# One block for the four mixer heads, and state space rows issued ahead

## The reference, cut to what matters

```
cum     = cumsum(dt * a)
h_new   = h * exp(cum[-1]) + B^T (exp(cum[-1] - cum) * xdt)
seg     = exp(where(lower, cum_i - cum_j, -inf))
y       = (C B^T * seg) xdt + (C h) * exp(cum)
```

```
rq, rk, rv, rg, gq, gk, gv, gz, ga, gb, gate_a, gate_b = split(xm @ w_in)
y_ret = silu(rg) * rms_norm(retention(rope(rq), rope(rk), rv))
q, k, v = silu(causal_conv(cat(gq, gk, gv), conv_w));  q, k = l2(q), l2(k)
A     = strict_lower(beta k k^T * decay) + I
per chunk:  v_new = A^-1 (beta v - beta exp(g) k S);  o = q exp(g) S + (q k^T * decay) v_new
            S = S * exp(g_last) + (k exp(g_last - g))^T v_new
y_gdn = rms_norm(o, norm_w) * silu(gz)
out   = (sigmoid(gate_a) * y_ret + sigmoid(gate_b) * y_gdn) @ w_out
```

## Time and profile before

| | us |
|---|---|
| median of three runs | 4228.22 |
| the profiled execution, own time | 4227.81 |
| its span, first to last instruction | 4225.5 |
| stage of the mixer heads, 2828.1 to 3604.9 | 776.8 |
| state space stage, from 1123 to 1718 | 595 |

### The profile page before, as it was taken

How to read it: one execution, slowest core, us unless ns; L and a number is a source line. 1 busy time by engine, 2 the same in 40 slices (tenths; PEclk the granted TensorE clock), 3 DMA queues, 4 the chain that set the end, 5 groups by cost and what they waited for, 6 DMA issues and landing times. The chain is left out here.

```text
span 4225.5 us, 56473 instructions
## 1 busy us (share of the span) xinstructions
PE 3428.7 (81%) x23892; PEld 2063.1 (49%) x23892; DVE 1546.8 (37%) x3163; ACT 916.8 (22%) x1817; POOL 53.6 (1%) x72
## 2 busy tenths in 40 slices
PE   5799999998698988699748787848888887659994
PEld 1466666666555544344333232334444444358883
DVE  2466666666345756100140000031413233241112
ACT  1243344342134446100110000011111212001001
POOL 0000000000000000000000000000000000000000
PEclk7899999999799998799859999959899999859997
DMA  3112212221222211420149999340111110247873
GB/s 135 46 56 71 71 56 71 71 70 55 73 70 68 67 63 50 176 100 0 73 187 391 428 428 428 142 164 3 80 40 42 40 43 0 85 158 293 326 317 150
DMA packets 109172, 548.20 MB, mean 130 GB/s; under 512 B 34336, under 2 KB 37136, under 8 KB 84512
## 3 DMA queue, kind: packets, MB, share of 16 engines
q1 hardware_dynamic: 102048, 519.97, 31.9%
q0 software_dynamic: 4608, 16.78, 1.1%
q10 hardware_dynamic: 2304, 8.39, 0.5%
HBM read 517.63 MB, written 27.47 MB: 129 GB/s over the span
## 5 line engine op out<-in xcount | busy, mean ns | idle before, releaser
L2066 PE MATMUL ex_ps<-ex_ring,ex_xs 128*64 128x512 f32 x1024 | 246.7, 639 | 62.1 <-DMA ex_ring<-expert_slabs_in 59.1
L571 PE MATMUL rw_ps<-hT,rw_w 128*128 128x512 f32 (+1 forms) x640 | 259.4, 535 | 16.4 <-DMA rw_w<-rw_slabs_in 16.1
L2803 PEld LDWEIGHTS ge_ps<-ge_xeT,ge_ring 128*128 128x128 f32 x2048 | 233.0, 193 | 10.5 <-issue 10.5
L2803 PE MATMUL ge_ps<-ge_xeT,ge_ring 128*128 128x128 f32 x2048 | 233.2, 276 | 2.9 <-DVE ge_xeT L2861 2.9
L2300 PE MATMUL mh_ps<-mh_w,xmT 128*128 128x512 f32 x512 | 221.5, 593 | 8.6 <-ACT mh_sg L2323 8.6
L2066 PEld LDWEIGHTS ex_ps<-ex_ring,ex_xs 128*64 128x64 f32 x1024 | 88.4, 147 | 219.9 <-issue 219.9
L1375 PE MATMUL sg_ps<-hTp,sg_w 128*128 128x512 f32 x384 | 174.4, 608 | 8.5 <-DMA sg_par<-conv_pars_in 8.5
L571 PEld LDWEIGHTS rw_ps<-hT,rw_w 128*128 128x128 f32 x640 | 113.4, 193 | 100.1 <-issue 73.8
L2300 PEld LDWEIGHTS mh_ps<-mh_w,xmT 128*128 128x128 f32 x512 | 97.0, 190 | 132.5 <-issue 120.5
L2291 PE MATMUL mh_ps<-xmT,mh_w_ahead 128*128 128x512 f32 x256 | 120.8, 636 | 22.8 <-PEq L61 22.8
L2066 PE MATMUL ex_ps<-ex_ring,ex_hidT 128*64 128x512 f32 x512 | 118.5, 617 | 14.2 <-DMA ex_ring<-expert_slabs_in 13.1
(11 more groups left out here) (568 smaller groups left out, 5538.8 us busy)
## 6 DMA issues: line engine op xcount, KB each, us to landing
ex_ring<-expert_slabs_in SPq DMA_DIRECT2D x96, 2048.0 KB, 19.8
ge_ring<-expert_slabs_in SPq DMA_DIRECT2D x48, 2048.0 KB, 12.3
rw_mod_w<-mod_w_in SPq DMA_DIRECT2D x64, 384.0 KB, 4.1
rw_mod_w<-ada_in SPq DMA_DIRECT2D x64, 256.0 KB, 3.3
sg_kern<-cum_dram SPq DMA_DIRECT2D x64, 256.0 KB, 3.2
mh_w_ahead<-head_slabs_in SPq DMA_DIRECT2D x8, 2048.0 KB, 10.0
mh_w<-head_slabs_in SPq DMA_DIRECT2D x8, 2048.0 KB, 10.0
rw_w<-rw_slabs_in SPq DMA_DIRECT2D x8, 1536.0 KB, 6.8
```

The source lines that it names most:

```text
L571: mm = pe.matmul(where[j, part], w[:, k, P * j:P * j + P], tokens, start=k == 0, stop=k == KC - 1)
L2066: mm = pe.matmul(ps[halves[j], bank, :], src[:, k, halves[j]], ring[:, (n + j) % RING, k, :], start=k == 0, stop=k == KC - 1)
L2803: mm = pe.matmul(ps[:, 2 + 2 * (j % 2) + n, P * f:P * f + P], w[:, k, P * f:P * f + P], xeT[:, j, k, :], start=k == 0, stop=k == KC - 1)
```

## The change

Two places.

In `ssm_branch` SP issues the first gate slab and the first five rows ahead of the passes. In pass c at step n it issues row 16c + n + 5 (the first whose buffer is then free), and the gate slab behind the row of step 1. Store and weight blocks keep their steps in the list.

`mixer_heads` becomes one block for the four heads; `mixer_head`, the hardware loop and the class `Inverse` are gone. Semaphores count on from head to head. The slabs go through a ring of two buffers. The arithmetic is the same; its order on the engines is new:
- token blocks alternate with turns, spread, products, scores and retention, so these are in the dense projection;
- the inverse has two pieces of two channel matmuls of the next head in each level, and the states have one such piece in each chunk; the taps for them are on VectorE in levels 3 to 6 (one behind the masks, one behind the subtracts), in chunk 2 and behind chunk 3;
- the gates are taken per token block, Silu, then Sigmoid;
- root and norm of the retention are ahead of the inverse; the norm row times the gate is between inverse and states;
- decay columns are read from `tok` without a copy; channel blocks use PSUM banks 5 and 6.

```diff
@@ ssm_branch, SP @@
+                sp.dma_start(wz[:, :, :], z_slabs[0]).then_inc(s.wz_in, 16)
+                for m in range(RING):
+                    load_rows(m)
                 for c in range(-1, SSM_G):
                     p = c + 1
-                    if p < SSM_G:
-                        if p:
+                    for n in range(16):
+                        if c >= 0 and 16 * c + n + RING < 16 * SSM_G:
+                            load_rows(16 * c + n + RING)
+                        if 0 < p < SSM_G and n == 1:
                             sp.wait_ge(s.z_done, nl * p)
-                        sp.dma_start(wz[:, :, :], z_slabs[p]).then_inc(s.wz_in, 16)
-                    for n in range(16):
-                        if c >= 0:
-                            load_rows(16 * c + n)
+                            sp.dma_start(wz[:, :, :], z_slabs[p]).then_inc(s.wz_in, 16)
@@ mixer_heads, SP @@
+                for n in range(2, 4 * HEADS):
+                    h, part = (n - 2) // 4, (n - 2) % 4
+                    if part == 0:
+                        sp.wait_ge(s.channel_major, 4 * h + 4)
+                    else:
+                        sp.wait_ge(s.token_major, 12 * h + 4 * part)
+                    sp.dma_start(w[:, n % 2, :, :], slabs[n]).then_inc(w_in[n % 2], 16)
+                    if part == 2 and h + 1 < HEADS:
+                        sp.wait_ge(s.scores_kept, 4 * h + 4)
+                        sp.dma_start(dec[:, :], decay[h + 1]).then_inc(s.dec_in, 16)
@@ TensorE @@
+                def channel(h, lo, hi):
+                    for j in range(lo, hi):
+                        b, k = j // KC, j % KC
+                        if j == 0 and h:
+                            pe.wait_ge(w_in[0], 32 * h)
+                            pe.wait_ge(s.token_kept, 12 * h)
+                        if k == 0 and b >= 2:
+                            pe.wait_ge(s.convolved, 4 * h + b - 1)
+                        mm = pe.matmul(ps[:, 5 + b % 2, :], w[:, 0, k, P * b:P * b + P], xmT[:, k, :], start=k == 0, stop=k == KC - 1)
+                        if k == KC - 1:
+                            mm.then_inc(s.channel_major, 1)
+                def invert(h, level):
...
+                        mm.then_inc(x_turned[k], 1)
+                    if more:
+                        channel(h + 1, 4 * level - 4, 4 * level - 2)
...
+                        mm.then_inc(y_product[k], 1)
+                    if more:
+                        channel(h + 1, 4 * level - 2, 4 * level)
...
+                        mm.then_inc(z_product[k], 1)
+                def chain(h, c):
...
+                    pe.matmul(ps[:, 1, 0:DV], mats[:, 0, c, :], rhs[:, :], start=True, stop=True).then_inc(s.v_done, 1)
+                    if h + 1 < HEADS:
+                        channel(h + 1, 24 + 2 * c, 26 + 2 * c)
+                    pe.wait_ge(s.v_ready, CH2 * h + c + 1)
...
+                channel(0, 0, 4 * KC)
+                for h in range(HEADS):
+                    token(h, 0)
+                    turn_channels(h)
+                    for n in range(1, 4):
+                        token(h, n)
+                    for n in range(3):
+                        turn(h, n)
+                    token(h, 4)
+                    turn(h, 3)
+                    turn(h, 4)
+                    token(h, 5)
+                    spread(h)
+                    token(h, 6)
+                    products(h)
+                    token(h, 7)
+                    scores(h, 0)
+                    scores(h, 1)
+                    token(h, 8)
+                    scores(h, 2)
+                    scores(h, 3)
+                    token(h, 9)
+                    retain(h, 0)
+                    retain(h, 1)
+                    token(h, 10)
+                    retain(h, 2)
+                    retain(h, 3)
+                    token(h, 11)
+                    pe.wait_ge(s.ret_kept, CH2 * h + CH2)
+                    for level in range(1, LEVELS_UP):
+                        invert(h, level)
+                    for c in range(CH2):
+                        chain(h, c)
@@ ScalarE, from the gates of block 9 on @@
+                    retain_square(h, 0)
+                    retain_square(h, 1)
+                    gates(h, 10)
+                    retain_square(h, 2)
+                    retain_square(h, 3)
+                    act.wait_ge(s.mean_r, h + 1)
+                    act.activation(ss2[:, 0, :], ss2[:, 0, :], ACT.Sqrt).then_inc(s.root_r, 1)
+                    gates(h, 11)
+                    for level in range(1, LEVELS_UP):
+                        for k in range(2):
+                            act.wait_ge(x_turned[k], N * h + level)
+                            act.copy(xx[:, k, :], ps[:, 2 * k, 0:2 * P]).then_inc(x_ready[k], 1)
+                        if more and level == 5:
+                            silu(h + 1, 0)
+                    if more:
+                        silu(h + 1, 1)
...
+                    act.activation(ss2[:, 1, :], ss2[:, 1, :], ACT.Sqrt).then_inc(s.root_g, 1)
+                    if more:
+                        silu(h + 1, 2)
+                        silu(h + 1, 3)
@@ VectorE @@
+                    for level in range(1, LEVELS_UP):
+                        level_up(h, level)
+                    dve.wait_ge(s.gated, 8 * h + 8)
+                    link(dve.tensor_tensor(gate_g[:, :, :], gate_g[:, :, :], per_unit(norm_w, CH2), ALU.mult))
+                    for c in range(CH2):
+                        chain(h, c)
+                        if more and c == 2:
+                            for i in range(4):
+                                tap(h + 1, 2, i)
+                    if more:
+                        for i in range(4):
+                            tap(h + 1, 3, i)
```

More of the change, by code:

```diff
@@ L328, in shift @@
         link(dve.scalar_tensor_tensor(out[:, 0:n - 1], u[:, 1:n], mu1, out[:, 0:n - 1], ALU.mult, ALU.add))
[L331 to L407, removed]
-            for k, g in self.slots(r):
-                act.wait_ge(self.x_turned[k], n * r + level)
-                act.copy(self.xx[:, k, self.cols], self.ps[:, 2 * k, self.cols]).then_inc(self.x_ready[k], 1)
-            if filler:
-                filler(level)
@@ L2279, in _ @@
+        og, oret = sb("mh_og", [P, CH2, DV]), sb("mh_or", [P, CH2, DV])
+        ps = keep.enter_context(nc.psum_tensor("mh_ps", [P, 8, 512], F32))
+        with stage(nc) as (s, block, _):
+            both = lambda name: [s.named(f"{name}{k}") for k in range(2)]
+            w_in, xt_ready, x_turned, x_ready = both("w_in"), both("xt_ready"), both("x_turned"), both("x_ready")
+            y_product, y_masked, z_product = both("y_product"), both("y_masked"), both("z_product")
             @block.sync
@@ L2280, in _ @@
             def _(sp):
[L2281 to L2285 removed]
+                sp.dma_start(par[:, :, :], taps.rearrange("h p b n -> p h (b n)")).then_inc(s.par_in, 16)
@@ new lines, in spread, with products @@
+                def spread(h):
+                    pe.wait_ge(s.turns_kept, 5 * h + 3)
+                    for bank, a in ((1, 0), (2, 7)):
+                        for c in range(CH2):
+                            mm = pe.matmul(ps[:, bank, P * c:P * c + P], at(h, a, c).broadcast_to([P, P]), cst("tri_f"), start=True, stop=True)
+                    mm.then_inc(s.cum_spread, 1)
+                def products(h):
+                    pe.wait_ge(s.turns_kept, 5 * h + 5)
+                    for c in range(CH2):
+                        mm = pe.matmul(ps[:, PAIR_BANK[c // 2], 256 * (c % 2):256 * (c % 2) + 256], turned[:, 0, P * c:P * c + P], kq[:, c, :], start=True, stop=True)
+                    mm.then_inc(s.products, 1)
@@ new lines, in scores, with retain @@
+                def scores(h, j):
+                    if j < 2:
+                        pe.wait_ge(s.cum_taken, 2 * h + 2)
+                    else:
+                        pe.wait_ge(s.scores_kept, 4 * h + j - 1)
+                    pe.matmul(ps[:, 1 + j % 2, 0:SEQ - P * j], turned[:, 2, P * j:P * j + P], turned[:, 1, P * j:SEQ], start=True, stop=True).then_inc(s.scores, 1)
+                def retain(h, i):
+                    pe.wait_ge(s.mats_ready, 4 * h + 4)
+                    pe.wait_ge(s.scores_kept, 4 * h + i + 1)
+                    for j in range(i + 1):
+                        mm = pe.matmul(ps[:, PAIR_BANK[i // 2], DV * (i % 2):DV * (i % 2) + DV], sc[:, j, P * (i - j):P * (i - j) + P], vr[:, j, :], start=j == 0, stop=j == i)
+                    mm.then_inc(s.ret_done, 1)
@@ new lines, in level_up @@
+                def level_up(h, level):
+                    for k in range(2):
+                        dve.wait_ge(y_product[k], N * h + level)
+                        dve.tensor_tensor(units(yy[:, k, :]), units(ps[:, 2 * k, :]), per_unit(cst(f"low{level}"), 2), ALU.mult).then_inc(y_masked[k], 1)
+                    if h + 1 < HEADS and level >= 3:
```

(8 more changed lines are left out.)

545 lines of the change are left out of this document (283 added, 262 removed).

## The result

| | us, median | range | runs |
|---|---|---|---|
| before | 4227.9 | 4226.3 to 4228.6 | 4 |
| after | 4062.9 | 4059.4 to 4068.0 | 4 |

The ratio is 0.9611, 95% interval [0.9594, 0.9628]: 165 us less, where 4062 was predicted. The profiled execution took 4064.2 us (span 4062.3), and TensorE was granted 0.904 of full speed over it, 0.892 before.

What follows compares the result with a forecast made beforehand. TensorE was busy 81% of the span, so time is won only where it stands still or is slow. From 4228.2 us, 130 off for the heads and 36 for state space rows gave 4062, range 4040 to 4094.

Steps and rivals of the forecast that it cites:

- token part: A head's token blocks with turns, products, scores and retention between them: 82.4 + 13.8 + 0.3 = 96.5 us.
- inverse with fillers: A head's six inverse levels with channel matmuls of the next head in them, plus uncovered waits: 39.0 us.
- before the states, and states: VectorE's serial work before the states, 3.2 us, then three state chunks with fillers, 19.7 us.
- a head with a next one: Each of the first three heads, from token part through states with fillers: 158.4 us.
- last head: The fourth head, which has no fillers in inverse or states: 141.9 us.
- state space, saved: Rows issued earlier at group starts: 8 us less at group 0, 14 each at groups 1 and 2, 36 in all.
- first filler behind the gates: Start of the inverse: first filler writes banks the last gates must leave, a wait of 1.85 us.
- third chunk behind the taps: States: four taps on VectorE before the next right side, 3.1 us less 0.3 of slack; chunk takes 7.6.
- rival 1: State space rows give little, 5 us, as TensorE then waits for ScalarE: 4093 us; chance 0.07.
- Rival 2: Clock stays low in the woven inverse and states, 116 us more: 4178; chance 0.07, in part or whole (4100 to 4180).
- Rival 3: Stalls in the heads are smaller than charged, half of 14 us a head hidden: 4037 us; chance 0.05.
- Rival 4: Slab ring of two starves the heads' projection, making it slower: 4272 us at 45 us from release; chance 0.01.

Runs made afterwards that it cites:

- e6: Changed kernel with VectorE's four taps moved from the third chunk of the states, two each into chunks 0 and 1; 4052.0 us, ratio 0.9588.
- e7: Changed kernel with the last gate's sigmoid behind level 1's first copies, first filler waiting one gate block less, norm row behind level 2; 4047.3 us.
- e8: Changed kernel with the edits of both e6 and e7; 4035.9 us, ratio 0.9535.
- e2: Changed kernel's new heads with SyncE's old order of transfers in the state space stage; 4102.6 us, ratio 0.9703.
- e10: Changed kernel with turns, spread, products, scores and retention moved from between the token blocks to behind block 11, weaving kept; 4122.5 us.
- e4: Old kernel with state space rows issued ahead of the 2 MB gate slab but still behind the wait for the gate products; 4220.8 us, ratio 0.9978.
- e3: Changed kernel unwoven: next head's four channel blocks in one lump ahead of its token blocks, no fillers in inverse or states; 4063.9 us.
- e9: e3, the unwoven version, with the edit of e7 to last gate and norm row; 4055.0 us, ratio 0.9589.
- e5: Old kernel with gate-product wait and slab moved behind a group's first five rows, first slab behind no wait; 4194.7 us, ratio 0.9917.

## Why the prediction was right

**The sum.** Each piece against the step that predicted it:

| step | predicted | measured |
|---|---|---|
| head 0's channels and slow start | 29.9 | 29.8 |
| token part | 96.5 | 96.3 |
| inverse with fillers | 39.0 | 39.1 |
| before the states, and states | 22.9 | 24.3 |
| a head with a next one | 158.4 | 159.7, 162.4, 158.4 |
| last head | 141.9 | 141.2 |
| heads, stage | 647 | 651.5 |
| state space, saved | 36 | 36.5 |

The stage's 4.5 us of error are −0.1 at its start, +5.3 over three heads and −0.7 in the last, and runs of one kernel scatter by as much. The state space came out piece by piece as well: from the stage's start to group 1 it got 8.2 us shorter, where 8 was predicted for group 0. That 4062 was met to 1 us is in part luck: the heads gave 4.5 us less than predicted, some 2 came from stretches that nobody changed, and the same kernel's second measurement (a0) is 4067.1.

Of the signs that were named beforehand one failed narrowly: the second head took 162.4 us, where 155 to 162 was stated. The others came: no idle of TensorE over 3.0 us between the first and the last matmul of the heads, 59 more table loads in four heads, clock 1.00 in head 0's inverse, and at groups 1 and 2 no TensorE idle over 0.75 us and no wait of ScalarE for a row.

**Waits.** The first filler behind the gates: 1.85 predicted, 1.81. Ahead of the first solve: 3.2, and 2.97. The third chunk behind the taps: 2.8, and 2.96. The tap of level 5: 0.65, and 0.28. A level with fillers takes 6.17 us (from one level's product L2309 to the next, 2922.72 to 2928.89), 0.59 more than its matmuls, where 0.6 was charged. e6, e7 and e8 are the test of these: what each wait was put down to is taken away, and the wait ahead of the third chunk and the one of the first filler are gone, while the one ahead of the first solve falls from 2.96 to 1.71, by the norm row's 1.25.

**The term that was mis-sized** is the states with fillers, and it is the clock. The prediction took every filler at 1.72 us, start to start (a duration of 1.88), for its four instructions. Behind the waits of 2.95 to 2.97 us the fillers ran at full speed in some heads and at 1.2 GHz, wholly or in part, in others:

```profile
3121.00 3.46 PE L2229 MATMUL mh_ps<-xmT,mh_w_ahead 128*128 128x512 f32 x4
...
3139.00 1.22 PE L2331 MATMUL mh_ps<-mh_rhs,mh_mats 128*128 128x256 f32 x2 [2.95 <-DVE mh_rhs L2577]
3140.01 3.62 PE L2229 MATMUL mh_ps<-xmT,mh_w_ahead 128*128 128x512 f32 x4
```

That is the second head, the one of 162.4 us. In the third head both fillers took 1.88 us, and it measured 158.4 us, the predicted number: the 5.3 us of error over three heads are all in the two heads with slow fillers. Over the changed kernel's two profiles, e6 and e7 there are 18 such waits, and behind 12 of them the fillers took 2.7 to 3.6 us (in e2 behind 3 of 6, in e10 behind 6 of 6). Behind the 6 waits of 1.70 or 1.71 us of e7 and e8 they took 1.88 each time.

**The rivals.** The rows gave all they were charged (rival 1: 5 us; 36.5 measured), though e4 shows a trace of its mechanism: the waits for ScalarE ahead of the turns grew by 3.6 us, from 10.8 to 14.4. Rival 2 holds in the small: the clock did fall in the states, not at a cost of 116 us but of some 9 to 14 (e8 against the changed kernel's two profiles). In head 0's inverse, behind the 1.81 us at its start and with 0.59 us of standing still in each level, it was 1.00. The page named beside rival 2 (the Trainium skill, TensorE: Matmul & The Clock Gate, A second HAM failure mode: psum-queue depth-cycling) tells of another kernel whose clock swung with frequent micro-idles; the changed kernel's inverse, with an idle at every level and 1.00, does not show it. Rival 3 asked for half of the stalls to hide by themselves; they measured about what was charged, and e8 had to remove their causes. Rival 4 did not arise: a slab landed in 7.8 us (median of 14), and no wait of TensorE for a slab is in the profile of the heads.

**ScalarE's tables.** One gate block in the trace of ScalarE:

```profile
2859.78 0.39 ACT L2405 ACTIVATE mh_gr<-mh_ps 128x256 f32<-128x256 f32 x1 [3.46 <-PE mh_ps L2245]
2860.17 1.28 ACT L2408 ACT_TABLE_LOAD   x1
2861.47 0.39 ACT L2408 ACTIVATE mh_sg<-mh_ps 128x256 f32<-128x256 f32 x1
```

The load starts where the pass before it ends, the next pass starts 1.30 us after the load does, and all 64 loads of the two lines that alternate (L2405, L2408) take 1283 ns. The drain of 1.38 us per switch that the Trainium skill states (ScalarE: Activation LUTs, What ACT_TABLE_LOAD costs) does not show, and the 6 to 11 us that it would have added are not there: the wait in which they would stand measured 1.81 for the 1.85 that had been worked out without it.

**What the prediction did not say.** It added up one sum for the new heads and never asked which part of the change earned it. Its own rows would have told that weaving was worth little: 39.0 + 3.2 + 19.7 = 61.9 us woven. Without, the same rows give 27.5 for the channels, 20.2 for the levels and an estimate of 16 for the states (2.4 before the first solve, three chunks of 3.83, 1.9 to the last output), 63.7 in all. Where the 125 us come from is shown in part: 55 to 60 from turns, spread, products, scores and retention lying between token blocks (e10), 0 to 8 from weaving (e3). The remaining 60 to 70 were not tested by themselves. By the waits they are the barriers, 65 us less, but in the old order some of those barriers also held the scores' start, so this last split is a reading, not a result.

## What to carry to other kernels

Before weaving work into a serial chain, write down for each side engine what it must do between two steps of the chain; a filler that brings its own side work (here four taps, 3 us) can cost nearly as much as it fills until that work is put where the engine has slack (e8 against e9). A wait in an in-order DMA queue delays all that is issued behind it: look first for the smallest move that takes the needed transfers out from behind it. In e5 the buffers that already stood free then gave the rows their lead of 27.5 us. Price a wait of TensorE at its length plus the matmuls behind it at 1.2 GHz, when the rows show that waits of that length are followed by them.

## What the hardware showed beside

- The same wait of 2.96 us, in the same place of three like heads, was followed by fillers at 1.88 or at up to 3.62 us, differently from head to head and run to run. The changed kernel's heads differ by 4.0 us (158.4 to 162.4), and e8's, with no such wait, by 0.04. What decides it in one case or the other stays open.
- It is not a matter of waits of 3 us alone. In e7 and e8 the fillers behind 1.7 us ran at full clock, six times of six. In e3, whose inverse has no fillers, a product (L2312) behind a wait of 1.98 us took 1.71 us for the 1.16 that it takes in e9, where the waits are 0.24 and 0.58.
- A table load runs ahead of the wait of the instruction that needs it. After the load at 2862.84 ScalarE's silu of the next block started at 2867.52 behind TensorE, with no load in between, so between the token blocks alternating tables cost TensorE nothing, as ScalarE had 6.9 us for 3.4 of work, even with ScalarE busy 216 us of the stage instead of 140. Behind the last block nothing covers the load: its 1.28 us are part of the 1.81 that the first filler waits.
